# State-space heads of the first two layers: 128-token tiles in five phases, or 64-token blocks in one phase

## The chip, the cores and the metric

The kernel runs on one core of a Trainium2 chip. The metric is the device time of one execution in microseconds (us). Three executions of the kernel before took 3934.63 to 3938.2 us, median 3936.54 us. PE is the matrix engine, PEld its weight load; DVE, ACT and POOL are the vector, scalar and GpSimd engines.

## The reference, cut to what matters

The program is a four-layer network on 512 tokens of width 1024, in float32. Layers 0 and 1 mix tokens with six state-space heads, a dilated attention and a 31-tap convolution; the change lies in the state-space heads:

```python
def step(state, inp):              # per token and head; state is 64 x 64
    r_t, w_t, k_t, v_t, a_t, b_t = inp     # a = -kk, b = kk * a
    sa = einsum('bhij,bhj->bhi', state, a_t)
    state = state * w_t[:, :, None, :] + sa[..., None] * b_t[:, :, None, :] + v_t[..., None] * k_t[:, :, None, :]
    y_t = einsum('bhij,bhj->bhi', state, r_t)
    return state, y_t
# then per head: y = (y - mean) * rsqrt(var + eps) * ln_w + ln_b + bonus, times a gate
```

The kernels do it in chunks of 64 tokens. Within a chunk the effect of sa on later tokens is the inverse of a unit triangular 64 x 64 matrix, made of repeated squares and updates; between chunks a state is carried.

## The kernel before, in words

Everything is laid out with features on the 128 partitions (two heads of 64 above each other, e = 0 and 1) and tokens along the free axis; three such pairs (cc = 0 to 2) hold the six heads. `first_mixers` is called twice, once per layer, between the long weight chains, and runs one phase after another. A phase is a block in which each engine has its own list of instructions, tied by semaphores; it ends when all engines have ended.

After `rwkv_scale` (L1154: per pair a scan over tokens, the exponentials of the decays, the scaling of r, k, a, b) come, for each pair, a phase of transposes (`transposes`, L723) and one of `rwkv_pair` (L1219). The latter works on tiles of 128 tokens, in which two chunks lie, and on one head at a time: `by_tile` (L1256) is four matmuls of 128x128x128, the other head's rows being zeroed in the stationary operand (`heads_apart`, L1214) and the other chunk masked away. Scores, three rounds of squares and updates, two corners (m32, m64) and the products with the values follow each other, with DVE and ACT copying out of PSUM between them. Then `rwkv_states` (L1410) carries the state of all three pairs over eight chunks, two products and six DVE instructions each, and `rwkv_output` (L1476) makes y, its mean and variance per head and the output.

The convolution runs beside this. ACT multiplies a shifted input by one tap (`conv_terms`, L1586) and POOL adds the term to a sum (`conv_sums`, L1601): 62 taps, of which 60 are added by POOL. ACT's term k waits until POOL has added term k-4. Before, the taps are split over the three `rwkv_pair` phases, and the normalization of the convolution lies in `rwkv_states`.

A float32 matmul stands in the trace as two records, each with its weight load: `rwkv_output` issues 24 matmuls at L1489 per layer, and the trace has 48 rows. The orders below count matmuls, the trace records.

Of the kernel before, what the change touches and what calls it, by code (L numbers as in the profile page):

```python
# [12 lines left out]
ALU = mybir.AluOpType  # L13
# [4 lines left out]
P = 128  # L18
# [18 lines left out]
SHIFTED = 10  # L37
NGC = T // GC
# [4 lines left out]
def columns(widths):  # L43
# [17 lines left out]
    ("m16", P), ("m32", P), ("m64", P), ("m16T", P), ("strictT", P), ("inclT", P), ("incl32T", P), ("dist", T),  # L61
# [4 lines left out]
def constants():  # L66
# [12 lines left out]
    always = [np.eye(P), np.ones((P, P)), same(HD), col(1e-6), col(1e-12), col(64e-5), col(1e-5), col(1.0)]  # L79
    mixers = [  # L80
        below * same(16), below * (same(32) - same(16)), below * (same(64) - same(32)), (below * same(16)).T,
        (below * same(64)).T, upto * same(64), upto * same(32), dist,
# [114 lines left out]
class Core:  # L197
# [15 lines left out]
    N_TEMPS = align(NCB)  # L213
# [940 lines left out]
    def rwkv_scale(self):  # L1154
# [7 lines left out]
        names = ("chain", "sums_ready", "exps_ready", "bonus_in", "bonus_sum", "chunk_done")  # L1162
        with self.phases.phase(*names) as (block, chain, sums_ready, exps_ready, bonus_in, bonus_sum, chunk_done):
# [50 lines left out]
    def heads_apart(self):  # L1214


        return [self.pj(19), self.pj(20)], [self.pj(21), self.pj(22)], [self.mix[:, 0, :], self.mix[:, 1, :]]

    def rwkv_pair(self, cc):  # L1219

# [6 lines left out]
        fa, fb, fr, fk = self.pj(10 + cc), self.pj(13 + cc), self.pj(cc), self.pj(3 + cc)  # L1227
        At, Kt, Vt = (self.units("ring", i, 1)[:, 0, :] for i in range(3))
        Bt = self.units("arena", cc, 1)[:, 0, :]
        tok = lambda u: u.rearrange("p (n f) -> p n f", f=P)  # L1230
        self.transposes([g for src, dst in ((fa, At), (fk, Kt), (self.pj(6 + cc), Vt), (fb, Bt))
                         for g in self.to_tokens([src], tok(dst))])
        buffers = [[self.units("h", i, 1)[:, 0, :] for i in range(8)], [self.units("ring", 3 + i, 1)[:, 0, :] for i in range(8)]]
        (L, LT, L2, L2T, I, IT, O32, O64) = zip(*buffers)
        UT, W, MV = (self.units("arena", u, 1)[:, 0, :] for u in (3 + cc, 9 + cc, 33))
        KV = self.units("arena", 12 + 2 * cc, 2)
        G = self.units("arena", 18 + 2 * cc, 2)
        RKV = self.units("arena", 24 + cc, 1)[:, 0, :]
        rows = [slice(0, HD), slice(HD, P)]
        FB, FA, FK = self.heads_apart()  # L1240
        RKT = [self.units("arena", 32, 1)[:, 0, :], self.mix[:, 2, :]]
        tile = lambda u, i: u[:, i * P:(i + 1) * P]
        wide = lambda name: self.c(name, P).unsqueeze(1).to_broadcast([P, NT, P])
        names = ("scores_l", "masked_l", "masked_corners", "started", "scores_a", "scores_b", "masked_a", "masked_b", "values", "values_read",
                 "squares", "squares_copied", "updates", "updated", "corner", "corner_copied", "ends", "ends_read",
                 "by_head", "turned", "turned_copied", "term_ready", "added")
        with self.phases.phase(*names) as (block, scores_l, masked_l, masked_corners, started, scores_a, scores_b, masked_a, masked_b, values, values_read,
                                           squares, squares_copied, updates, updated, corner, corner_copied, ends, ends_read,
                                           by_head, turned, turned_copied, term_ready, added):
            @block.gpsimd  # L1250
            def _(pool):
                self.conv_sums(pool, self.conv_part(cc, RW), term_ready, added)

            @block.tensor
            def _(pe):
                def by_tile(bank, lhs, rhs, r=slice(0, P), out=slice(0, P)):  # L1256
                    for i in range(NT):
                        mm = nc.tensor.matmul(tile(banks[bank][out, :], i), tile(lhs[r, :], i), tile(rhs[r, :], i), start=True, stop=True)
                    return mm
                pe.wait_ge(by_head, 6)  # L1260
                for e in range(2):
                    by_tile(0 + e, FB[e], fa)
                    by_tile(2 + e, FA[e], fb).then_inc(scores_l, 1)
                for e in range(2):
                    by_tile(4 + e, FK[e], fa)
                    by_tile(6 + e, FB[e], fr).then_inc(scores_a, 1)
                pw = [(L, LT), (L2, L2T)]
                pe.wait_ge(masked_l, 2)
                for n in range(3):
                    (p, pt), (q, qt) = pw[n % 2], pw[(n + 1) % 2]  # L1270
                    if n:
                        pe.wait_ge(squares_copied, 4 * n)
                    for e in range(2):
                        if n == 0 and e == 1:
                            pe.wait_ge(masked_corners, 2)
                        mm = by_tile(0 + 2 * e, pt[e], p[e])
                        if n < 2:
                            mm = by_tile(1 + 2 * e, p[e], pt[e])
                        mm.then_inc(squares, 1)
                    if n == 0:  # L1280
                        for e in range(2):
                            pe.wait_ge(masked_a, e + 1)
                            by_tile(4 + e, FK[e], fr).then_inc(scores_b, 1)
                        pe.wait_ge(masked_b, 2)
                        for e in range(2):
                            for i in range(NT):
                                nc.tensor.matmul(banks[6][:, i * P + e * HD:i * P + e * HD + HD], tile(I[e], i),
                                                 tile(Vt, i)[:, e * HD:e * HD + HD], start=True, stop=True)
                        for i in range(NT):
                            for e in range(2):  # L1290
                                mm = nc.tensor.matmul(tile(banks[4][rows[e], :], i), tile(Vt, i)[:, e * HD:e * HD + HD],
                                                      tile(RKT[e], i), start=True, stop=True)
                        mm.then_inc(values, 1)
                        pe.wait_ge(started, 2)
                    pe.wait_ge(squares_copied, 4 * n + (4 if n < 2 else 2))
                    if n:
                        pe.wait_ge(updated, 2 * n)
                    for e in range(2):
                        by_tile(5 + 2 * e, q[e], IT[e]).then_inc(updates, 1)
                pe.wait_ge(updated, 6)  # L1300
                pe.wait_ge(values_read, 2)
                for e in range(2):
                    for i in range(NT):
                        mm = nc.tensor.transpose(tile(banks[4 + 2 * e], i), tile(IT[e], i), self.c("ident", P))
                    mm.then_inc(turned, 1)
                for e in range(2):
                    by_tile(e, O32[e], IT[e]).then_inc(corner, 1)
                pe.wait_ge(corner_copied, 2)
                pe.wait_ge(turned_copied, 2)
                for e in range(2):  # L1310
                    by_tile(4 + 2 * e, L[e], I[e])
                    by_tile(5 + 2 * e, I[e], L[e]).then_inc(updates, 1)
                pe.wait_ge(updated, 8)
                for e in range(2):
                    by_tile(e, O64[e], IT[e]).then_inc(corner, 1)
                pe.wait_ge(corner_copied, 4)
                for e in range(2):
                    by_tile(5 + 2 * e, I[e], L[e]).then_inc(updates, 1)
                pe.wait_ge(updated, 10)
# [936 lines left out]
```

## Time and profile before

| | us |
|---|---|
| median of three executions | 3936.54 |
| the profiled execution: its time, its span | 3933.45, 3931.7 |
| state-space part of layer 0 (`rwkv_scale` to the end of `rwkv_output`) | 266.7 |
| the same of layer 1 | 266.7 |
| of these in layer 0: scale / three pairs with transposes / states / output | 21.6 / 174.9 / 38.8 / 31.4 |

The parts follow each other without overlap, and nothing of the weight chains runs beside them, so a stage is read as a stretch of time: its length, the busy time of each engine and the clock granted to TensorE (1.00 is 2.4 GHz, 0.50 is 1.2 GHz).

### The profile page before, as it was taken

What the parts mean: (1) busy time and instruction counts of PE and PEld (TensorE: products, weight loads), DVE (VectorE), ACT (ScalarE), POOL (GpSimd) and SP (SyncE); (2) the same over time, 40 slices, a digit from 0 to 9 for tenths busy, and PEclk for the clock granted to TensorE, in tenths of its full rate; (3) what the DMA queues carried; (4) which work ended last, traced back from release to release, by engine and by line L of the source; (5) the groups of instructions that cost most, each with busy time, mean ns of one, the idle gap of its engine ahead of it and who ended that gap; (6) DMA issues with size and microseconds to landing.
All of it is one profiled execution on the core that took longest, in us unless ns stands there. A gap on an engine that the chain in (4) does not pass through costs nothing. (4 is left out here: it accounts for less than half of the span.)

```text
span 3931.7 us, 45649 instructions
## 1 busy us (share of the span) xinstructions
PE 3550.2 (90%) x17442; PEld 2914.3 (74%) x17442; DVE 1867.7 (48%) x2852; ACT 1309.2 (33%) x1921; POOL 324.5 (8%) x259
## 2 busy tenths in 40 slices
PE   7999976869999999995877999986899997789998
PEld 5888855758888888873766888865788876568887
DVE  4443335455443444335445444433566444656652
ACT  3222433423222322424433322313422331453231
POOL 0000323400000000042420000000000000210000
PEclk9999988979999999997988999995899998899999
DMA  3332300002232223320002223320222333012232
GB/s 112 97 101 92 113 12 1 1 35 97 96 105 88 96 96 103 112 71 1 1 1 68 94 98 103 122 74 1 73 98 97 100 104 121 1 44 95 98 102 81
DMA packets 73440, 295.09 MB, mean 75 GB/s; under 512 B 8144, under 2 KB 9168, under 8 KB 72144
## 3 DMA queue, kind: packets, MB, share of 16 engines
q1 hardware_dynamic: 73296, 293.09, 22.4%
q8 instruction: 101, 1.65, 0.2%
q14 instruction: 43, 0.35, 0.0%
HBM read 290.96 MB, written 2.10 MB: 75 GB/s over the span
## 5 line engine op out<-in xcount | busy, mean ns | idle before, releaser
L427 PE MATMUL bank<-src_hi,tile_hi 128*128 128x512 f32 x2720 | 1068.7, 393 | 26.2 <-DVE tile_lo L501 25.4
L428 PE MATMUL bank<-src_lo,tile_hi 128*128 128x512 f32 x2720 | 1059.3, 389 | 0.0
L429 PE MATMUL bank<-src_hi,tile_lo 128*128 128x512 f32 x2720 | 1059.2, 389 | 0.0
L501 DVE TENSOR_TENSOR tile_lo<-raw_tiles,tile_hi 128x1024 fp32r<-128x1024 f32 (+1 forms) x484 | 618.7, 1304 | 84.3 <-ACT tile_hi L453 68.1
L427 PEld LDWEIGHTS bank<-src_hi,tile_hi 128*128 128x128 f32 x2720 | 511.0, 188 | 138.7 <-DVE tile_lo L501 25.4
L428 PEld LDWEIGHTS bank<-src_lo,tile_hi 128*128 128x128 f32 x2720 | 511.2, 188 | 110.4 <-issue 5.3
L453 ACT ACTIVATE tile_hi<-raw_tiles 128x1024 fp32r<-128x1024 f32 (+1 forms) x484 | 524.6, 1112 | 199.0 <-DMA raw_tiles<-in_w_in 92.8
L429 PEld LDWEIGHTS bank<-src_hi,tile_lo 128*128 128x128 f32 x2720 | 511.1, 188 | 106.7
L427 PE MATMUL bank<-hid_hi,tile_hi 128*128 128x512 f32 x1312 | 515.1, 393 | 48.4 <-DVE tile_lo L501 48.4
L428 PE MATMUL bank<-hid_lo,tile_hi 128*128 128x512 f32 x1312 | 514.0, 392 | 0.0
L429 PE MATMUL bank<-hid_hi,tile_lo 128*128 128x512 f32 x1312 | 513.5, 391 | 0.0
L427 PEld LDWEIGHTS bank<-hid_hi,tile_hi 128*128 128x128 f32 x1312 | 248.5, 189 | 102.1 <-DVE tile_lo L501 50.5
L428 PEld LDWEIGHTS bank<-hid_lo,tile_hi 128*128 128x128 f32 x1312 | 248.7, 190 | 52.0
L429 PEld LDWEIGHTS bank<-hid_hi,tile_lo 128*128 128x128 f32 x1312 | 248.5, 189 | 52.2
L701 DVE TENSOR_TENSOR temps<-bank,temps 128x512 f32<-128x512 f32 x88 | 60.8, 691 | 405.5 <-PE bank L429 405.5
L668 DVE SCALAR_TENSOR_TENSOR x_res<-bank,x_res 128x512 f32<-128x512 f32 (+1 forms) x80 | 55.3, 691 | 414.1 <-PE bank L429 414.1
L687 ACT ACTIVATE temps<-temps 128x512 f32<-128x512 f32 x88 | 55.6, 632 | 574.9 <-DVE temps L701 574.9
L660 ACT ACTIVATE src_hi<-temps 128x512 fp32r<-128x512 f32 (+1 forms) x72 | 45.5, 632 | 554.7 <-DVE temps L672 554.7
L536 DVE TENSOR_TENSOR big<-bank,hspace 128x512 f32<-128x512 f32 x76 | 52.6, 692 | 248.9 <-PE bank L429 231.5
L1612 POOL TENSOR_TENSOR mix<-mix,masks 128x512 f32<-128x512 f32 x120 | 148.7, 1271 | 221.7 <-ACT masks L1599 221.7
L716 DVE TENSOR_TENSOR hid_lo<-temps,hid_hi 128x512 f32 (+1 forms) x132 | 91.4, 693 | 119.0 <-ACT hid_hi L691 119.0
L689 ACT ACTIVATE temps<-temps,par 128x512 f32<-128x512 f32 x44 | 31.9, 724 | 289.4 <-DVE temps L711 289.4
(380 smaller groups left out, 3569.9 us busy)
## 6 DMA issues: line engine op xcount, KB each, us to landing
raw_tiles<-in_gu SPq DMA_DIRECT2D x264, 512.0 KB, 3.4
raw_tiles<-in_down SPq DMA_DIRECT2D x96, 704.0 KB, 4.1
raw_tiles<-in_w_in SPq DMA_DIRECT2D x46, 512.0 KB, 3.4
masks<-in_masks SPq DMA_DIRECT2D x4, 2108.0 KB, 8.3
raw_tiles<-in_w_out SPq DMA_DIRECT2D x16, 512.0 KB, 3.5
raw_tiles<-in_a_in SPq DMA_DIRECT2D x16, 512.0 KB, 3.5
raw_tiles<-in_w_mem SPq DMA_DIRECT2D x16, 512.0 KB, 3.4
raw_tiles<-in_a_out SPq DMA_DIRECT2D x8, 512.0 KB, 3.8
```

The source lines that it names most:

```text
L427: nc.tensor.matmul(bank, wh, hi[:, kk, 0:p.n], start=(kk == 0), stop=False)
L428: nc.tensor.matmul(bank, wh, lo[:, kk, 0:p.n], start=False, stop=False)
L429: mm = nc.tensor.matmul(bank, wl, hi[:, kk, 0:p.n], start=False, stop=last and (p.kind == "gated" or s == p.h - 1))
L453: nc.scalar.activation(self.tile_hi[:, t, 0:kc * P], self.tile_raw[:, t, 0:kc * P], ACT.Copy).then_inc(hi_ready, 1)
L501: v.tensor_tensor(self.tile_lo[:, t, 0:kc * P], self.tile_raw[:, t, 0:kc * P], self.tile_hi[:, t, 0:kc * P].bitcast(F32), ALU.subtract).th ...
L536: v.tensor_tensor(p.dst[:, p.place(i), 0:p.n], p.banks_of(banks, k)[0], self.rstd_of(p), ALU.mult).then_inc(bank_free, 1)
L660: nc.scalar.activation(chunk(self.src_hi, i), self.temps[:, 4 + k % 2, :], ACT.Copy).then_inc(own["next_hi"], 1)
L668: v.scalar_tensor_tensor(chunk(self.x, i), p.banks_of(self.banks, k)[0], float(p.factor), chunk(self.x, i), ALU.mult, ALU.add).then_inc(ow ...
L687: nc.scalar.activation(one, one, ACT.Silu).then_inc(own["activated"], 1)
L701: v.tensor_tensor(gate, bank[0], rstd, ALU.mult).then_inc(own["gate_ready"], 1)
L716: v.tensor_tensor(chunk(self.hid_lo, i), prod, chunk(self.hid_hi, i).bitcast(F32), ALU.subtract).then_inc(own["hid_ready"], 1)
L1612: self.nc.gpsimd.tensor_tensor(acc[:, c, :], acc[:, c, :], slots[k % 4], ALU.add).then_inc(added, 1)
```

## The change

`rwkv_pair`, `rwkv_states` and `rwkv_output` and the transposes between them become one phase, `rwkv_chunks`. All work is on blocks of 64 tokens and 64 features. A product is 16 matmuls of 64x64x64 (8 chunks, 2 heads); the first head uses partitions 0 to 63 of input and output, the second 64 to 127, so they lie in different quarters of the array. PE's list interleaves the first head of a product with the second head of the product before it, chunk by chunk, in different PSUM banks. 33 named products are made for each of the three pairs, pair after pair within a name; 27 of them share a ring of five banks, where a product waits until the copy of the fifth before it is made. 13 names are copied out by ACT, the rest by DVE: 19 groups of three full-width instructions, among them the copies of the turned squares (sq2t, sq4t) and of the score-weighted values (mv). Squares with the identity take the place of the transposes. The carried state is six steps (`step`), each three matmuls per head half and one DVE addition. POOL first scales b, k and the identity by the decay at the chunk's end (9 instructions), then adds taps. 16 taps (14 additions) are moved ahead into `rwkv_scale`, the other 46 lie in the new phase, three or four after each ACT group. The convolution's normalization moves behind the last product. The masks are 64 wide instead of 128.

```diff
+FIRST_TAPS = 16
...
-    ("m16", P), ("m32", P), ("m64", P), ("m16T", P), ("strictT", P), ("inclT", P), ("incl32T", P), ("dist", T),
+    ("m16", CH), ("m32", CH), ("m64", CH), ("m16T", CH), ("strictT", CH), ("inclT", CH), ("ident2", CH), ("incl32T", P), ("dist", T),
...
+        taps = self.conv_part(0, FIRST_TAPS)
...
-                for pair in self.heads_apart():
-                    for e in range(2):
-                        nc.gpsimd.memset(pair[e][(1 - e) * HD:(2 - e) * HD, :], 0.0)
+                self.conv_sums(pool, taps, term_ready, added)
...
+                    self.conv_terms(act, taps, 6 * c, 6, term_ready, added)
...
+    RWKV_PRODUCTS = ("lt", "l", "v", "a", "sq2", "sq2t", "ka", "up1", "sq4", "sq4t", "mv", "up2", "sq8", "g", "up3", "rk", "turn", "c1",
+                     "b", "up4", "up4t", "k", "c2", "up5", "n1", "u", "w", "q", "mt", "n2", "y1", "y2", "y3")
+    RWKV_VECTOR = ("lt", "l", "started", "o32", "o64", "sq2t", "ka", "up1", "sq4t", "mv", "up2", "g", "up3", "rk", "up4", "up4t", "up5", "q", "mt")
+    RWKV_SCALAR = ("v", "a", "sq2", "sq4", "sq8", "turn", "c1", "b", "k", "c2", "u", "w", "n2")
+
+    def rwkv_chunks(self):
...
+        ring = [(name, cc) for name in self.RWKV_PRODUCTS if name not in ("l", "n1", "n2", "y1", "y2", "y3") for cc in range(RW)]
+        bank_of = {at: banks[i % 5] for i, at in enumerate(ring)}
...
+        taps = self.conv_part(FIRST_TAPS, TAPS * CV)
...
+                for cc in range(RW):
+                    nc.gpsimd.tensor_tensor(chunks(Be[cc]), chunks(Fb[cc]), end(cc), ALU.mult).then_inc(ends_scaled, 1)
+                    nc.gpsimd.tensor_tensor(chunks(Ke[cc]), chunks(Fk[cc]), end(cc), ALU.mult).then_inc(ends_scaled, 1)
+                    nc.gpsimd.tensor_tensor(chunks(MT[cc]), mask("ident2"), end(cc), ALU.mult).then_inc(ends_scaled, 1)
+                self.conv_sums(pool, taps, term_ready, added)
...
+                def half(at, lhs, rhs, e, c):
+                    first = at[0] not in ("n2", "y2", "y3")
+                    r = rhs[rows[e], :] if rhs.shape[1] == CH else chunk(rhs, c)[rows[e], :]
+                    return nc.tensor.matmul(chunk(bank_of[at], c)[rows[e], :], chunk(lhs, c)[rows[e], :], r,
+                                            start=first and c == 0, stop=(c == NCH - 1), skip_group_check=True)
+
+                def product(name, cc, lhs, rhs, skip=0):
+
+                    nonlocal behind
+                    at = (name, cc)
+                    if at in ring and ring.index(at) >= 5:
+                        last = ring[ring.index(at) - 5]
+                        if last[0] in self.RWKV_SCALAR:
+                            pe.wait_ge(kept_a, in_a(*last))
+                        else:
+                            pe.wait_ge(kept_v, in_v(*last))
+                    for c in range(NCH):
+                        if c >= skip:
+                            half(at, lhs, rhs, 0, c)
+                        if behind is not None and c >= behind[3]:
+                            mm = half(*behind[0:3], 1, c)
+                    if behind is not None:
+                        mm.then_inc(multiplied, 1)
+                    behind = (at, lhs, rhs, skip)
...
+                def step(e, c):
+
+                    if c > 1:
+                        pe.wait_ge(added_to[e], c - 1)
+                    for cc in range(RW):
+                        mm = nc.tensor.matmul(scan_banks[e][rows[e], cc * CH:(cc + 1) * CH], chunk(MT[cc], c)[rows[e], :],
+                                              N[rows[e], cc, (c - 1) * CH:c * CH], start=(cc == 0), stop=(cc == RW - 1), skip_group_check=True)
+                    mm.then_inc(stepped[e], 1)
...
+                for cc in range(RW):
+                    pe.wait_ge(kept_v, in_v("l", cc))
+                    product("sq2", cc, LT[cc], L[cc])
+                for cc in range(RW):
+                    product("sq2t", cc, L[cc], LT[cc])
...
+                for c in range(1, NCH - 1):
+                    for e in range(2):
+                        step(e, c)
+                    if c <= 2:
+                        product("y1", c, V[c], RK[c])
+                    elif c <= 5:
+                        product("y2", c - 3, L2T[c - 3], G[c - 3])
...
+                    product("y3", cc, states_behind(cc), Fr[cc], skip=1)
+                finish()
+                self.conv_mean(pe, taps, added, conv_mean)
...
+                def keep(name, to):
...
+                        act.wait_ge(multiplied, made(name, cc))
+                        nc.scalar.activation(to[cc], bank_of[name, cc][:, :], ACT.Copy).then_inc(kept_a, 1)
+                    more = 3 if name in ("v", "a", "sq2") else 4
+                    self.conv_terms(act, taps, term, more, term_ready, added)
...
+                def copied(name, to):
+                    for cc in range(RW):
+                        dve.wait_ge(multiplied, made(name, cc))
+                        v.tensor_copy(to[cc], bank_of[name, cc][:, :]).then_inc(kept_v, 1)
...
+                copied("sq2t", L2T)
...
+                copied("sq4t", LT)
+                copied("mv", KA)
...
+                        to = N[rows[e], :, c * CH:(c + 1) * CH]
+                        v.tensor_tensor(to, to, scan_banks[e][rows[e], 0:RW * CH].rearrange("p (c f) -> p c f", c=RW), ALU.add).then_inc(added_to[e], 1)
...
-        for cc in range(RW):
-            self.rwkv_pair(cc)
-        self.rwkv_states()
-        self.rwkv_output()
+        self.rwkv_chunks()
```

PE's list at the start of layer 0's work on the heads, before (`hspace` holds the first head's matrices, `ring` the second's):

```order
L1258 MATMUL bank0<-big_66 128x128 [waits by_head_10]
L1258 MATMUL bank0<-big_66 128x128 x3
L1258 MATMUL bank2<-big_66 128x128 x4
L1258 MATMUL bank1<-big_66 128x128 x4
L1258 MATMUL bank3<-big_66 128x128 x4
```

and PE's list at the same place after (`big` holds the inputs of both heads):

```order
L1279 MATMUL bank0<-big_66 64x64 x8
L1279 MATMUL bank1<-big_66 64x64
L1279 MATMUL bank0<-big_66 64x64
L1279 MATMUL bank1<-big_66 64x64
L1279 MATMUL bank0<-big_66 64x64
L1279 MATMUL bank1<-big_66 64x64
```

Whole runs of four 128-wide matmuls into one bank have become 64-wide ones that alternate between two banks, one head half each.

PE's list in the carrying of the state, before, two chunks of it (L1435 multiplies by the state, L1445 updates it):

```order
L1435 MATMUL bank0<-arena_63 64x128 [waits loaded_1]
L1435 MATMUL bank0<-arena_63 64x128 x2
L1445 MATMUL bank2<-ring_65,arena_63 128x128 [waits tile_split_3]
L1445 MATMUL bank2<-ring_65,arena_63 128x128 x2
L1435 MATMUL bank1<-arena_63 64x128 [waits loaded_1]
L1435 MATMUL bank1<-arena_63 64x128 x2
L1445 MATMUL bank3<-ring_65,arena_63 128x128 [waits tile_split_3]
L1445 MATMUL bank3<-ring_65,arena_63 128x128 x2
```

PE's list there after, one step of both head halves (the 16 matmuls of an output product stand between two such steps; bank1 and bank2 hold the halves):

```order
L1313 MATMUL bank1<-arena_63,ring_65 64x64 [waits src_hi_ready_3]
L1313 MATMUL bank1<-arena_63,ring_65 64x64
L1313 MATMUL bank1<-arena_63 64x64
L1313 MATMUL bank2<-arena_63,ring_65 64x64 [waits src_ready_3]
L1313 MATMUL bank2<-arena_63,ring_65 64x64
L1313 MATMUL bank2<-arena_63 64x64
```

Two dependent groups per chunk have become one.

## Rows read from the trace of the kernel before

**Rows 1.** The page: busy time, share of the span, instructions; TensorE's clock in 40 slices.

```profile
PE 3550.2 (90%) x17442; PEld 2914.3 (74%) x17442; DVE 1867.7 (48%) x2852; ACT 1309.2 (33%) x1921; POOL 324.5 (8%) x259
PEclk9999988979999999997988999995899998899999
```

**Rows 2.** Stages: from:to, length, busy us (records) by engine; clock; DMA.

```profile
core 0: us, PE busy (x) PEld busy (x) DVE busy (x) ACT busy (x) POOL busy (x), PEclk, DMA share, GB/s
593.40:615.00 21.60, 6.22 (x6) 1.50 (x6) 21.45 (x36) 5.00 (x9) 3.31 (x6) 0.50 0.00 0
615.00:673.10 58.10, 47.68 (x392) 45.28 (x392) 24.34 (x40) 23.81 (x40) 22.33 (x18) 0.94 0.00 1
789.90:828.70 38.80, 24.90 (x98) 17.07 (x98) 25.85 (x48) 7.78 (x9) 0.00 (x0) 0.66 0.00 0
828.70:860.10 31.40, 20.62 (x108) 16.91 (x108) 10.55 (x15) 7.97 (x11) 0.00 (x0) 0.66 0.00 1
593.40:860.10 266.70, 193.48 (x1388) 170.01 (x1388) 132.38 (x219) 93.95 (x151) 77.61 (x66) 0.84 0.00 1
1835.70:2102.40 266.70, 193.49 (x1388) 168.55 (x1388) 132.39 (x219) 94.09 (x152) 77.67 (x66) 0.84 0.00 1
```

**Rows 3.** Timeline of PE: start, length of the run, instruction, records.

```profile
641.39 1.95 PE L1258 MATMUL bank<-hspace 128*128 128x128 f32 x16
...
2070.35 10.48 PE L1489 MATMUL bank<-big,arena 128*128 128x64 f32 x48 [0.92 <-PEq L113]
2080.76 5.32 PE L1494 MATMUL bank<-arena,ring 128*64 128x128 f32 x48
...
2681.13 6.71 PE L1803 MATMUL bank<-arena 32*64 32x128 f32 x128 [1.05 <-PEq L113]
...
544.61 0.49 PE L962 MATMUL bank<-big 64*128 64x128 f32 x4
```

**Rows 4.** Timeline of PE, single records in two column halves.

```profile
669.82 0.27 PE L1326 MATMUL bank<-hspace,ring 128*64 128x128 f32 x1
669.83 0.27 PE L1326 MATMUL bank<-ring 128*64 128x128 f32 x1
669.93 0.27 PE L1326 MATMUL bank<-hspace,ring 128*64 128x128 f32 x1
```

**Rows 5.** PE alone in stretches: length, busy us (records), clock, DMA.

```profile
640.00:670.00 30.00, 24.22 (x206) 1.00 0.00 1
2070.30:2080.80 10.50, 10.45 (x50) 0.50 0.00 0
2683.20:2687.70 4.50, 4.50 (x76) 0.50 0.00 0
```

**Rows 6.** Timelines of DVE, ACT and POOL in layer 0.

```profile
628.04 0.68 DVE L1372 TENSOR_TENSOR hspace<-bank,masks 128x512 f32<-128x512 f32 x1
628.64 0.68 DVE L1373 TENSOR_TENSOR hspace<-bank,masks 128x512 f32<-128x512 f32 x1
...
791.33 0.55 DVE L1456 TENSOR_TENSOR ring<-bank,arena 64x384 f32<-64x384 f32 x1 [0.96 <-PE bank L1435]
...
645.66 2.55 ACT L1599 ACTIVATE masks<-arena,par 128x512 f32<-128x512 f32 x4
...
810.43 1.28 ACT L1651 ACT_TABLE_LOAD   x1
...
646.45 9.87 POOL L1612 TENSOR_TENSOR mix<-mix,masks 128x512 f32<-128x512 f32 x8 [6.22 <-ACT masks L1599]
```

**Rows 7.** Timelines of ACT, DVE, PE: the ends of `rwkv_scale` and `rwkv_output`.

```profile
611.08 0.61 ACT L1178 ACTIVATE hspace<-hspace 128x512 f32<-128x512 f32 x1
...
614.26 0.68 DVE L1212 TENSOR_TENSOR arena<-bank,big 128x512 f32<-128x512 f32 x1
...
859.30 0.69 DVE L1533 TENSOR_TENSOR mix<-hspace,big 128x512 f32<-128x512 f32 x1
...
844.01 2.41 PE L1500 MATMUL bank<-hspace,const 128*128 128x512 f32 x5
```

More of the change, by code:

```diff
@@ L1264, in _ @@
[L1264 to L1319, printed above, removed]
@@ L1327, in _ @@
-                for o in range(2):
-                    for i in range(NT):
-                        mm = nc.tensor.matmul(tile(banks[2 + o], i), tile(Kt[rows[o], :], i), tile(Vt[rows[o], :], i), start=True, stop=True)
-                mm.then_inc(ends, 1)
+                behind = None
+                def half(at, lhs, rhs, e, c):
[3 more added lines that the diff above has]
+                                            start=first and c == 0, stop=(c == NCH - 1), skip_group_check=True)
@@ new lines, in finish @@
+                def finish():
+                    nonlocal behind
+                    for c in range(behind[3], NCH):
+                        mm = half(*behind[0:3], 1, c)
+                    mm.then_inc(multiplied, 1)
+                    behind = None
+                def step(e, c):
[5 more added lines that the diff above has]
+                    mm.then_inc(stepped[e], 1)
@@ L1358, in _ @@
-                act.wait_ge(ends, 1)
-                nc.scalar.activation(UT, banks[0][:, :], ACT.Copy)
-                nc.scalar.activation(W, banks[1][:, :], ACT.Copy).then_inc(ends_read, 1)
+                term = 0
+                def keep(name, to):
+                    nonlocal term
+                    for cc in range(RW):
+                        act.wait_ge(multiplied, made(name, cc))
+                        nc.scalar.activation(to[cc], bank_of[name, cc][:, :], ACT.Copy).then_inc(kept_a, 1)
+                    more = 3 if name in ("v", "a", "sq2") else 4
+                    self.conv_terms(act, taps, term, more, term_ready, added)
+                    term += more
@@ new lines, in _ @@
+                keep("v", V)
+                keep("a", A)
+                keep("sq2", L2)
+                keep("sq4", L)
+                keep("sq8", L2)
+                keep("turn", L2T)
+                keep("c1", L)
+                keep("b", B)
+                keep("k", K)
+                keep("c2", L2)
+                keep("u", L)
+                keep("w", L2T)
+                keep("n2", [N[:, cc, :] for cc in range(RW)])
+                assert term >= len(taps)
+                self.conv_squares(act, conv_centred, conv_squared)
@@ new lines, in increased @@
+                def increased(name, to, old, ready):
+                    for cc in range(RW):
+                        dve.wait_ge(multiplied, made(name, cc))
+                        if ready is not None:
+                            dve.wait_ge(kept_v, in_v(ready, cc))
+                        v.tensor_tensor(to[cc], old[cc], bank_of[name, cc][:, :], ALU.add).then_inc(kept_v, 1)
+                masked("lt", LT, "m16T")
+                masked("l", L, "m16")
+                for cc in range(RW):
+                    dve.wait_ge(kept_v, in_v("lt", cc))
+                    v.tensor_tensor(chunks(IT[cc]), chunks(LT[cc]), mask("ident2"), ALU.add).then_inc(kept_v, 1)
@@ L1579, in _, with conv_part @@
                     nc.vector.tensor_copy(lora[r, k, :], self.par1[r, PC1["lora"]:PC1["lora"] + RW * P])
[L1581 to L1584 removed]
+    def conv_part(self, first, last):
+        return [(j, c) for j in range(TAPS) for c in range(CV)][first:last]
     def conv_terms(self, act, taps, first, n, term_ready, added):
```

408 lines of the change are left out of this document (180 added, 228 removed).

## The prediction

> **What bounds the kernel now.** I read the page first, then the stages, then the timelines of PE at the kinds of matmul that the change is made of, and last the ends of the stages on the other engines. The page shows PE busy in 90% of the span [rows 1]; most of that is weight products that the change does not touch. The stages show where it acts: from the start of the scaling to the end of the output 266.7 us in either layer, 533 in all, with nothing of the weight chains beside it [rows 2]. A microsecond saved there is one saved in the total. Within them, one pair with its transposes takes 58.1 us, PE busy in 47.7 of it, DVE in 24.3, ACT in 23.8, POOL in 22.3: PE bounds it, with gaps where it waits for copies. In the carrying of the state (38.8 us) PE and DVE are each busy for 25 us: a chain of hops [rows 2]. The clock granted is 0.94 in the pair, 0.66 in the two stages behind it, 0.50 in the scaling.
>
> **What PE's small matmuls cost.** A float32 matmul is two records. At L1258 16 records of a 128-wide stationary and 128 moving columns take 1.95 us at full clock [rows 3, 5], 0.112 each; a product for one head over 512 tokens is four matmuls, 0.89 us, and 1.8 for both heads. At half clock, 48 records at L1489 with a 128-wide stationary and 64 moving columns take 10.48 us [rows 3, 5]: without the tail of the last, 0.214 each. Halving the moving side gains nothing there, the load sets the pace. At L1494 the same number, two column halves running together, takes 5.32 us [rows 3]: 0.21 per pair of records with 128 moving columns. The same pairs at full clock start 0.11 apart [rows 4].
>
> The new matmul is 64 wide on both sides. Half the load of L1489 gives 0.107 us per record at half clock, half the stream of L1494 gives the same; at full clock 0.053. The first head's quarter and the second's are interleaved. That such quarters run together is shown by L962, where two row halves alternate: four records in 0.49 us, of which a lone one takes about 0.27, so 0.22 for what would be 0.33 in file [rows 3]; and by L1803, 32x64 tiles with 128 moving columns, at 0.052 each [rows 3], a quarter of the 0.214 of a full record at that clock. So a product of 16 matmuls is 16 pairs of records: **1.71 us at half clock, 0.86 at full clock**. If the quarters did not overlap it would be 3.42 and 1.71.
>
> **Which clock.** This decides. The dense stream at L1489, PE busy 10.45 of 10.5 us, stays at 0.50 to its end; that at L1803, busy all of 4.5 us, too [rows 5]. Neither is a stream of 128-wide, 128-column matmuls. The products of that kind at L1258 hold 1.00 though PE is busy in only 24.2 of 30 us [rows 5]. The new stream resembles the first two (64 columns, partial tiles), and begins behind the scaling, at 0.50 [rows 2]. I take half clock throughout the phase.
>
> The Trainium skill, "TensorE: Matmul & The Clock Gate", section "Why this matters for your kernels", asks only that TensorE be kept busy without gaps for the full clock. By that rule the new phase, dense on PE, would run at 2.4 GHz; the two dense stretches at 0.50 in this trace disagree, and I follow them. It is the first rival.
>
> **The change part by part, for one layer.**
> - *Scaling.* POOL's memsets go (hidden, at nothing); 14 additions come, eight take 9.87 us [rows 6], so 17.3. The first can start when ACT has made its terms behind the first exponentials, about 599.5, so POOL ends near 617; DVE ends at 614.9 [rows 7]. Cost +2.2. ACT's terms (six are 3.8 us at 2.55 for four [rows 6]) fit between the exponentials. PE starts the new phase at 617.5.
> - *Products up to n2.* 30 names for three pairs, 90 products, and one slot more since a product's second half goes beside the next: 91 x 1.71 = 155.6. What lies beside: DVE 19 groups of three at a pitch of 0.60 [rows 6], 34 us, among them the nine copies sq2t, sq4t and mv, 5.4 us; ACT 39 copies and 46 terms at no more than 0.64, 54 us; POOL 9 scalings and 46 additions at 1.24, 68 us, which holds ACT back through the wait on term k-4. All are under half of 155.6, so they cost nothing at this clock; the tightest place, c2 behind four terms, stalls PE by half a microsecond. The last copy by ACT follows at 617.5 + 155.6 + 1 = 774.
> - *Carrying.* A step is 6 records in each quarter, 0.64, and with the output product behind it 2.35; five of them 11.8, which hides DVE's additions (64x384 takes 0.55 [rows 6], these have half the columns, some 0.35 each). The sixth stands alone: 0.64 and latency and two additions, 1.8. Then y3, seven chunks, three and the rest: 6.6. The last product is made at 774 + 11.8 + 1.8 + 6.6 = 794.
> - *End.* Before, the end of the products to the last write took 844.0 to 860.0 [rows 7], 16.0. Now the convolution's mean and variance are queued between (two and two matmuls of 512 columns on PE, about 2 us at half clock) and its Ln and Exp with two table loads of 1.28 [rows 6], 3.9 on ACT ahead of the heads' own. 16 + 5.9 = 22. The end is at 816.
> - *Gone:* six changes of phase, the transposes, the zeroing copies; they are in the stretch replaced.
>
> So 860.1 becomes 816, 44 less; both layers 88. Against the profiled execution 3933.45 - 88 = 3845; the median lies 3.1 above it, 3848. For stalls that I do not see I add 2: **3850 us**. The masks are narrower by 320 columns of 4216; their load runs beside the projection and is taken at nothing.
>
> The new kind of record stands nowhere in this trace. Its bounds by the nearest rows: 0.052 per record in file (L1803's pace for each single record would be 1.66 per product, nearly the same as chosen), at best 0.053 per pair, at worst 0.214 per pair. I take 0.107.
>
> The Trainium skill, "TensorE: Matmul & The Clock Gate", section "Wait — 56ns, not 53.3ns?", knows a floor of about 62 ns per matmul when its decoding runs in microcode. By it 32 records would be 2.0 us a product and each layer some 30 us longer, 3910 in all. L1803's 128 records in 6.71 us are under this floor, so the sum does not use it.
>
> **Rivals.**
> 1. *Full clock, in whole or part.* For it: PE has no gaps; L1494 is also a pair of partial tiles, and the 512-column records behind it take 0.48 each [rows 7], near four times the 0.107 of 128 columns at full clock, so the clock rose in it. Against it: the two stretches at 0.50. Then 91 x 0.856 = 78; POOL's 68 are just under it and ACT's waits for POOL begin to show. Carrying 6 x 1.2, y3 3.3, end 20: the layer ends near 728, 132 less; total 3936.5 - 264 = 3673. With half the phase at either clock 3760.
> 2. *The quarters do not overlap* (slower than before). The place is every product: e = 0 and e = 1 take turns. 3.42 a product adds 155.6 up to n2 and some 15 behind it: the layer ends at 986, 126 later than before, total 4188. It decides from 2.2 us a product on: (860 - 816)/91 = 0.48 above 1.71. For it: no row shows matmuls halved in rows and columns both, each quarter writing its own bank. Against it: L962 and L1803.
> 3. *A smaller cost in every record* (a floor between issues, stalls at the ring of banks): 10 to 25% on each product, 15 to 40 us a layer: 3880 to 3930, little or nothing gained.
>
> **How the numbers follow.** Forecast 0.58, own range 3825 to 3880. Rival 1 0.22 (half of it part-way, 3720 to 3825). Rival 3 0.10, rival 2 0.10. The range for eight in ten leaves out rival 2 and most of the fully fast case: 3690 to 3895. A measurement of this kernel tells 0.2%, 8 us. Faster is the forecast, rival 1 and most of rival 3: 0.87; the same 0.03; slower 0.10.
>
> **What would show it.** In the profile after: the clock row at 0.5 from the scaling to the end of the heads; the new matmul line at 32 records per 1.71 us; PE busy nearly all of 155 us, POOL done in the middle of the phase; the phase from 617.5 to 816. If the clock there is 1.0, rival 1 has it. If 32 records take over 2.2 us at half clock, rival 2 or 3. If PE waits for ACT's copies while ACT waits for POOL, I have the cover wrong. A difference outside the two stretches of heads would also make this wrong.

## The result, and the profile after

The changed kernel takes 3719.3 us (median of four runs, 3717.4 to 3720.2), the kernel before 3935.6 beside it: a ratio of 0.9449, 95% interval 0.9433 to 0.9466. The gain is 216 us where the forecast had 86 (3936 to 3850). The time is outside the forecast's own range (3825 to 3880) and inside the wide one (3690 to 3895); it lies between rival 1's two figures, 3673 for the full clock and 3760 for half of the phase at either, and the clock below is the full one. The step that failed is "I take half clock throughout the phase".

The page of the kernel after, engines and clock row (the lines of [rows 1]):

```profile
PE 3388.8 (91%) x21174; PEld 2781.2 (75%) x21174; DVE 1784.9 (48%) x2662; ACT 1283.4 (35%) x1879; POOL 347.9 (9%) x265
PEclk9999997989999999997989999967999997899999
```

PE executes 3732 records more and is busy 161 us less. POOL is busy 23 us more: 18 scalings of 1.04 us came and the memsets went, but the convolution's additions also took 160.6 us instead of 148.7 with a like number of them, which comes back below.

The stages of the kernel after, with the columns of [rows 2]: scaling; start of the products; products up to n2; carrying and output products; end; then the whole in either layer.

```profile
593.40:627.90 34.50, 6.22 (x6) 1.51 (x7) 33.50 (x36) 15.21 (x25) 22.65 (x14) 0.50 0.00 0
627.90:631.30 3.40, 3.38 (x49) 3.40 (x51) 0.00 (x0) 0.00 (x0) 3.12 (x4) 0.50 0.02 5
631.30:721.20 89.90, 85.97 (x2852) 84.49 (x2849) 38.66 (x57) 49.34 (x85) 61.55 (x51) 1.00 0.02 4
721.20:734.50 13.30, 12.51 (x337) 11.41 (x338) 6.29 (x15) 0.51 (x1) 1.27 (x1) 1.00 0.02 4
734.50:754.20 19.70, 6.95 (x17) 2.77 (x15) 10.96 (x16) 15.63 (x20) 0.00 (x0) 0.75 0.00 0
593.40:754.20 160.80, 115.03 (x3254) 103.58 (x3254) 89.41 (x124) 80.70 (x130) 88.59 (x69) 0.85 0.01 3
1731.00:1890.60 159.60, 114.53 (x3254) 103.98 (x3254) 89.59 (x124) 80.70 (x130) 90.10 (x69) 0.84 0.01 3
```

Three things are to be read here. The clock is 0.50 for the first 3.4 us of the products and 1.00 from there to the end of the output products. The scaling takes 34.5 us where [rows 2] had 21.6. And the stretch of 266.7 us is now 160.8 and 159.6; the two differences, 105.9 and 107.1, are 213 of the 215 us that the span lost, so nothing of weight happened elsewhere. Of layer 0's 105.9 us, 78.5 are busy time of PE (193.48 before, 115.03 now) and 27.4 its idle time. What the single phase brings without the 64-wide blocks was not run apart.

The pace of a product, from PE's timeline of single records in the middle of the phase (compare [rows 4]):

```profile
640.83 0.22 PE L1279 MATMUL bank<-masks,big 64*64 64x64 f32 x1
640.83 0.22 PE L1279 MATMUL bank<-arena 64*64 64x64 f32 x1
640.89 0.22 PE L1279 MATMUL bank<-masks,big 64*64 64x64 f32 x1
640.89 0.22 PE L1279 MATMUL bank<-arena 64*64 64x64 f32 x1
```

Two quarters, one of each head, start at the same moment and the next two some 0.058 us later (the rows round it to 0.06): they do run together, and 16 such pairs are 0.93 us a product.

Where the scaling lost its 13 us, VectorE's timeline in the second pair of heads:

```profile
601.30 1.65 DVE L1196 TENSOR_TENSOR_SCAN hspace<-masks,arena 128x512 f32<-128x512 f32 x1
602.87 1.42 DVE L1197 TENSOR_SCALAR hspace<-arena,par 128x512 f32<-128x512 f32 x1
604.20 1.75 DVE L1199 TENSOR_TENSOR hspace<-hspace,arena 128x512 f32<-128x512 f32 x1
605.87 0.68 DVE L1201 SCALAR_TENSOR_TENSOR big<-hspace,big 128x512 f32<-128x512 f32 x1
...
608.94 1.76 DVE L1210 TENSOR_TENSOR big<-big,hspace 128x512 f32<-128x512 f32 x1
610.62 1.75 DVE L1211 TENSOR_TENSOR big<-big,hspace 128x512 f32<-128x512 f32 x1
612.29 1.23 DVE L1212 COPY small<-hspace 128x8 f32<-128x8 f32 x1
613.44 0.68 DVE L1214 TENSOR_TENSOR arena<-bank,big 128x512 f32<-128x512 f32 x1
```

and GpSimd's in the same time:

```profile
599.04 6.36 POOL L1608 TENSOR_TENSOR mix<-mix,masks 128x512 f32<-128x512 f32 x4 [34.58 <-ACT masks L1595]
608.34 9.92 POOL L1608 TENSOR_TENSOR mix<-mix,masks 128x512 f32<-128x512 f32 x6 [2.94 <-ACT masks L1595]
```

A VectorE instruction of 512 columns with two inputs in SBUF takes 0.68 us while GpSimd is idle (605.4 to 608.3) and 1.75 while it adds; a copy of 8 elements takes 1.23. L1214, with one of its inputs in a PSUM bank, takes 0.68 while GpSimd adds. GpSimd's additions take 1.6 each instead of the 1.23 of [rows 6]. The Trainium skill, "SBUF — State Buffer", section "Who interferes with whom", says that a VectorE instruction with two SBUF inputs, or a copy or scalar operation in a two-port mode, and a GpSimd instruction that reads SBUF block each other for the length of an instruction. By that rule, which the prediction did not weigh, these steps had to wait; the trace agrees, with 0.4 (the scan) to 1.1 us more at a time.

### The profile page after: what moved, and what is told of

The parts are those of the page before. It is cut to its first block and busy times, and to the rows that moved or that the text cites. A ratio compares the mean times of both kernels' runs of the same rounds, so it can differ in the third digit from the quotient of the medians.

```text
span 3716.8 us, 52829 instructions
## 1 busy us (share of the span) xinstructions
PE 3388.8 (91%) x21174; PEld 2781.2 (75%) x21174; DVE 1784.9 (48%) x2662; ACT 1283.4 (35%) x1879; POOL 347.9 (9%) x265
## 5 line engine op out<-in xcount | busy, mean ns | idle before, releaser
L1608 POOL TENSOR_TENSOR mix<-mix,masks 128x512 f32<-128x512 f32 x120 | 160.6, 1375 | 134.9 <-ACT masks L1595 134.9
```

Source lines behind the costliest of these rows:

```text
L1608: self.nc.gpsimd.tensor_tensor(acc[:, c, :], acc[:, c, :], slots[k % 4], ALU.add).then_inc(added, 1)
```

## The experiments

The theories. **Clock:** a dense stream of these quarters, two in flight, brings TensorE to 2.4 GHz and keeps it there; the rows that the prediction followed are of another kind of stream. Its rival: [rows 5] showed stretches too short, or with too idle a past, for a rise. **Contention:** the 13 us of the scaling are VectorE and GpSimd in each other's way. Its rivals: the instruction's form, or something behind it. **Copies:** where the nine copies stand makes no difference. The edits are shown in short form. The kernel before of the first four runs took 3936.4 us; of the runs e5 to e8 3936.2; of the last two 3936.0.

**e5, the other kind, four times as long.** In the kernel before, ahead of the products at its line 1489:

```diff
+for _ in range(3):
+    for cc in range(RW):
+        for c in range(NCH):
+            matmul(banks[3 + cc][:, chunk c], state(c)[:, cc, :], pj(cc)[:, chunk c])
```

> The kernel before, with the 24 products of the output with a 128-wide stationary and 64 moving columns (48 records, 10.48 us at a granted clock of 0.50) made three times more in each layer, ahead of themselves, into free banks. If the kind of matmul keeps the clock at 0.50 (my step in the prediction), the 144 added records take 0.214 each: 31 us a layer, 3936 + 62 = 3998, and the granted clock stays 0.50 through some 42 us. If the stretch was only too short or its ahead too idle, the clock goes to 1.00 within it, a record then takes about 0.11, and the layer grows by 16 to 25 us: 3968 to 3986.

Measured in one run 3999.1 us, 63 more. PE's timeline and the clock in the stretch:

```profile
832.38 30.95 PE L1490 MATMUL bank<-big,arena 128*128 128x64 f32 x144 [0.92 <-PEq L113]
863.13 10.45 PE L1494 MATMUL bank<-big,arena 128*128 128x64 f32 x48
873.51 5.29 PE L1499 MATMUL bank<-arena,ring 128*64 128x128 f32 x48
```

```profile
840.00:850.00 10.00, 10.00 (x49) 10.00 (x48) 0.00 (x0) 0.00 (x0) 0.00 (x0) 0.50 0.00 0
...
860.00:870.00 10.00, 10.00 (x49) 10.00 (x48) 0.00 (x0) 0.00 (x0) 0.00 (x0) 0.50 0.01 2
870.00:880.00 10.00, 10.00 (x68) 9.06 (x68) 2.19 (x4) 0.00 (x0) 0.00 (x0) 0.57 0.00 0
```

PE is busy without a gap for 41 us at 0.50, and the clock rises only near the end of the column halves of L1499 behind it. So what the prediction said of L1489 was sound, and the length of that stretch was not its fault. The rule of the Trainium skill that the prediction weighed ("TensorE: Matmul & The Clock Gate", section "Why this matters for your kernels": busy without gaps gives the full clock) does not hold for this stream.

**e6, quarters in turn at the same place.**

```diff
+for _ in range(6):
+    for cc in range(RW):
+        for c in range(NCH):
+            for r in (rows 0:64, rows 64:128):
+                matmul(banks[3 + cc][r, chunk c], state(c)[r, cc, r], pj(cc)[r, chunk c])
```

> The kernel before, with 288 pairs of quarter matmuls (64 rows, 64 stationary and 64 moving columns, the two heads' quarters in turn, as the changed kernel's products) in each layer ahead of the output's products, into free banks; nothing reads them. If such a stream brings the clock up by itself, it does so within a few us here too, at the same place where the other kind stayed at 0.50; a pair then takes 0.058: 17 us a layer and the output's own 48 records go faster, 5 less: 3936 + 24 to 34 = 3965. If the rise in the changed kernel came from something else in its phase, the pairs stay at 0.107: 31 us a layer, 3998.

Measured in one run 3957.4 us, 21 more. PE's timeline, then the stretches with the clock:

```profile
828.98 19.00 PE L1492 MATMUL bank<-big,arena 64*64 64x64 f32 x576 [0.92 <-PEq L113]
847.90 5.57 PE L1496 MATMUL bank<-big,arena 128*128 128x64 f32 x48
853.41 2.84 PE L1501 MATMUL bank<-arena,ring 128*64 128x128 f32 x48
```

```profile
830.00:840.00 10.00, 10.00 (x296) 10.00 (x294) 0.00 (x0) 0.00 (x0) 0.00 (x0) 0.83 0.02 5
840.00:850.00 10.00, 10.00 (x293) 9.93 (x288) 0.00 (x0) 0.00 (x0) 0.00 (x0) 1.00 0.01 3
```

At the same place, behind the same stage, the quarters bring the clock up, and 576 records take 19.0 us where 144 of the other kind took 30.95. The L1496 behind them (L1489 of the kernel before) runs at 5.57 us instead of 10.48: already at full clock, it keeps it for that long. So at this place the kind of stream sets the clock, not the phase around it. The added time is below the expected 24 to 34. In a layer the pairs cost 19.0 where 17 were expected, and behind them 4.9 us at L1496, which was expected, and 2.0 at L1501, which was not, come off; 2.1 more come off outside the heads, where the matmuls of L1803 ran at full clock here (more on this below).

**e7, the same quarters in file.** In the changed kernel:

```diff
-for c in range(NCH):
-    half(at, lhs, rhs, 0, c)
-    half(*behind[0:3], 1, c)
+for c in range(NCH):
+    half(at, lhs, rhs, 0, c)
+for c in range(NCH):
+    half(*behind[0:3], 1, c)
```

> The changed kernel with the two heads' quarter matmuls of a product no longer in turn: all eight of the first head, then all eight of the second head of the product before. The numbers are the same. If the pace of 0.058 us for two quarters comes from their running together, a product takes 32 single records: 1.87 us at full clock instead of 0.93, 85 us a layer over 91 products and some 8 behind them, about 3905 in all; at half clock 3.4 us, and over 4150. If quarters run at 0.029 each in any order, nothing changes: 3719. Rival on the clock: with half the work in flight it falls to 0.50.

Measured 4060.1 us, ratio to the kernel before 1.0313 [1.0294, 1.0332]: slower than before. The first products, and two stretches, of its trace:

```profile
628.43 8.85 PE L1279 MATMUL bank<-big 64*64 64x64 f32 x96 [5.12 <-PEq L115]
```

```profile
634.00:660.00 26.00, 26.00 (x316) 26.00 (x315) 8.99 (x15) 4.22 (x7) 7.44 (x7) 0.50 0.01 1
755.00:785.00 30.00, 30.00 (x363) 30.00 (x361) 1.38 (x2) 10.89 (x19) 10.07 (x9) 0.50 0.01 2
```

The same instructions, in another order: in these stretches PE is never idle, the clock stays at 0.50 for over 200 us, a record starts every 0.084 us (16 of them between 723.91 and 725.25) and a product takes 2.68 us, 2.9 times the 0.93. A record in file at half clock costs less than the 0.107 that I had for a pair, so my 3.4 us a product, and over 4150, were too high; the sign of rival 2 was right for this order.

**e9, column halves of full height.** As e5, each added product cut into two matmuls on the column halves of its stationary, in turn.

```diff
+            for r in (slice(0, 64), slice(64, 128)):
+                matmul(banks[3 + cc][r, chunk c], state(c)[:, cc, r], pj(cc)[:, chunk c])
```

> As the kernel with the 24 products repeated three times (3999 us, clock 0.50 to the end, 31 us a layer), but each added product is two matmuls on the column halves of its stationary (128 rows, 64 wide, 64 moving columns), the halves in turn: 288 records instead of 144 for the same products. Since the quarters in turn rose to 1.00 and the same quarters in file stayed at 0.50, I expect that two tiles in flight are what brings the clock up, whether they share rows or not: 144 pairs at 0.107 for the first few us, then 0.058: 9 to 11 us a layer, and the 48 records behind them at full clock, 5 less: 3936 + 8 to 14 = 3947. The rival, that it is the halved rows: the pairs stay at 0.107, 15 us a layer, 3967; or halves of full height don't run together: 0.17 to 0.21 a pair and more, 3985 or above.

Measured in one run 3946.2 us, 10 more. PE's timeline:

```profile
833.38 10.99 PE L1491 MATMUL bank<-big,arena 128*64 128x64 f32 x288 [0.92 <-PEq L113]
844.30 5.57 PE L1495 MATMUL bank<-big,arena 128*128 128x64 f32 x48
```

The same products as e5's in 10.99 us instead of 30.95. Rows need not be split; two column halves in turn are enough.

**e10, the split alone.** The kernel before with its own 24 products at L1489 so split, nothing added.

```diff
-nc.tensor.matmul(banks[cc][:, chunk c], state(c)[:, cc, :], pj(cc)[:, chunk c])
+for r in (slice(0, 64), slice(64, 128)):
+    nc.tensor.matmul(banks[cc][r, chunk c], state(c)[:, cc, r], pj(cc)[:, chunk c])
```

> The kernel before with only its own 24 products of the output split in this way, nothing repeated: 10.48 us become 144 / 3 = 48 pairs, 5.1 at half clock or some 4 with the clock rising in it, and the 48 records behind them, 4.87 us before, start at full clock and take 2.8. So 6 to 8 us less a layer: 3936 - 14 = 3922. If the clock does not rise in it, 5 us a layer: 3926. If splitting does not help: 3936.

Measured 3916.7 us, ratio 0.9955 [0.9941, 0.9968]: 19 us less, by one more loop, and more than the 14 expected; 2.1 of them lie outside the heads, at the matmuls of L1803 (below). Its products, and the clock in them:

```profile
833.05 5.39 PE L1490 MATMUL bank<-big,arena 128*64 128x64 f32 x96 [0.92 <-PEq L113]
838.20 2.87 PE L1495 MATMUL bank<-arena,ring 128*64 128x128 f32 x48
```

```profile
833.10:838.20 5.10, 5.10 (x97) 0.50 0.01 3
```

The 10.47 us of L1489 in layer 0 became 5.39 at half clock: this part is the halves running together, not the clock. The clock rises at their end, and the records behind them take 2.87 us where they took 4.87.

**e1, no taps beside the scaling.** In the changed kernel FIRST_TAPS = 0, and four or five terms behind each group of ScalarE's copies instead of three or four.

```diff
-FIRST_TAPS = 16
+FIRST_TAPS = 0
-    more = 3 if name in ("v", "a", "sq2") else 4
+    more = 4 if name in ("v", "a", "sq2") else 5
```

> The 16 taps of the convolution that the changed kernel puts beside the scaling go into the products' phase (all 62 there, four or five terms behind each group of ScalarE's copies). Contention theory: VectorE's steps with both inputs in SBUF take 1.75 us instead of 0.68 because GpSimd adds at the same time; without its additions the scaling takes 21.7 us again and TensorE's first product starts near 616.5 instead of 627.9, so 11 us less in each layer, 3697 us in all. The rival, that the scaling is longer for another reason (its own new waits, ScalarE's terms behind the exponentials are gone too but cost only 3.8), gives a gain of 0 to 4 us a layer, 3712 to 3719. A second rival: GpSimd with 9 scalings and 62 additions (86 us in a phase of 93) holds the copies back and gives all of it back: 3719 or slower.

Measured 3706.5 us (ratio to before 0.9421 [0.9409, 0.9434]), 13 less than the changed kernel's 3719.3. VectorE at the rows shown above:

```profile
600.98 0.68 DVE L1199 TENSOR_TENSOR hspace<-hspace,arena 128x512 f32<-128x512 f32 x1
...
604.65 0.69 DVE L1210 TENSOR_TENSOR big<-big,hspace 128x512 f32<-128x512 f32 x1
...
605.85 0.17 DVE L1212 COPY small<-hspace 128x8 f32<-128x8 f32 x1
```

With GpSimd's additions gone, every step is back at its time, and VectorE's last step in the scaling starts 20.8 us after its first, as in the kernel before, instead of 33.3. But 22 us were expected and 13 came. PE's waits in the phase of layer 0 of e1 (us in total, times, longest) show where the rest went:

```profile
PE bank L1279 <- ACT arena L1431: 6.7, 5, 2.8
```

and its stretches with the clock:

```profile
656.00:670.00 14.00, 14.00 (x488) 14.00 (x484) 6.22 (x9) 7.65 (x14) 8.18 (x7) 1.00 0.02 5
670.00:684.00 14.00, 10.62 (x305) 10.40 (x301) 4.13 (x6) 10.03 (x17) 14.00 (x13) 0.88 0.01 2
684.00:698.00 14.00, 11.64 (x346) 11.50 (x342) 2.06 (x3) 9.57 (x16) 13.13 (x12) 0.88 0.02 4
```

PE waits for ScalarE's copies behind the longer groups of terms (2.1 us so in the changed kernel, 6.7 here), GpSimd is busy all the time, and in the stretches with gaps the granted clock is 0.88: a wait seems to be paid a second time through the clock.

**e4, the terms where nobody waits.** As e1, with the terms spread by hand.

```diff
-    more = 4 if name in ("v", "a", "sq2") else 5
+    more = TERMS_BEHIND[name]   # v 4, a 4, sq2 9, sq4 9, sq8 9, turn 0, c1 3, b 5, k 2, c2 5, u 2, w 6, n2 4
```

> As the kernel without taps beside the scaling, but the 62 terms stand where ScalarE is not followed by a copy that TensorE waits for: 9 each behind sq2, sq4 and sq8, none behind turn, two or three behind c1, k and u. If the stalls that remain in the products (15 us of issue time before the first matmul of a product in two layers, 10 for ScalarE's copies) are due to copies queued behind terms, 3 to 5 us a layer less than with the even spread: 3688 us. If GpSimd's 86 us are the bound, the spread changes nothing: as the first kernel, 3697.

Measured 3688.8 us (3687.7 to 3691.2), ratio to before 0.9377 [0.9364, 0.9390]: the fastest version here, 30.5 less than the changed kernel. The same wait and stretch in it:

```profile
PE bank L1281 <- ACT arena L1433: 1.5, 3, 0.8
```

```profile
670.00:684.00 14.00, 13.46 (x462) 13.33 (x459) 4.12 (x6) 10.26 (x19) 12.40 (x10) 1.00 0.02 5
```

Eighteen us lie between e1 and e4 with equal work on every engine, so GpSimd's 86 us of work, the second rival of e1's expectation, are not the bound. Of these nine us a layer, PE's waits for copies account for 5.8 (8.8 in e1, 3.0 here); that the rest is the lower clock is an estimate.

**e2, another form.** In the scaling, L1199, L1210 and L1211:

```diff
-v.tensor_tensor(r, r, e_in, ALU.mult)
+v.scalar_tensor_tensor(r, r, 1.0, e_in, ALU.mult, ALU.mult)
```

> Three TENSOR_TENSOR instructions a pair in the scaling (the sums before, r and k) become SCALAR_TENSOR_TENSOR with a factor of 1, same result; in the trace that form took 0.68 to 0.69 us beside GpSimd's additions. If the form decides who is slowed, some six of them come down from 1.75 to 0.69: 6 us less in each layer, 3707 us. If any step of VectorE with two SBUF inputs waits for the addition that GpSimd has begun, and the quick ones only stood where GpSimd was idle, nothing changes: 3719, and SCALAR_TENSOR_TENSOR is then seen at 1.7 us.

Measured 3718.0 us (3715.8 to 3720.4): no change. In its trace the new form is as slow where GpSimd adds:

```profile
603.63 1.75 DVE L1199 SCALAR_TENSOR_TENSOR hspace<-hspace,arena 128x512 f32<-128x512 f32 x1
...
608.37 1.75 DVE L1210 SCALAR_TENSOR_TENSOR big<-big,hspace 128x512 f32<-128x512 f32 x1
```

The theory of the form falls: the quick ones had stood where GpSimd was idle.

**e8, the taps beside the scaling in the kernel before.**

```diff
 def rwkv_scale: pool
+    pool.wait_ge(cleared, 6)
+    self.conv_sums(pool, taps[0:16], term_ready, added)
 def rwkv_scale: act, behind the exponentials of pair c
+    self.conv_terms(act, taps[0:16], 6 * c, 6, term_ready, added)
```

> The kernel before with this one part of the change: the first 16 taps of the convolution stand beside the scaling (terms on ScalarE behind the exponentials, 14 additions on GpSimd), and the three pairs share the other 46. If two engines reading SBUF in turn is what stretches the scaling, it does so here: 11 to 13 us a layer more ahead of the first pair. The pairs, in which TensorE sets the pace, gain at most a little from their fewer terms (0 to 3 us a layer): 3936 + 16 to 26 = 3952 to 3962. The rival, that in the changed kernel the scaling was longer for what is behind it, gives 3936 or less.

Measured 3960.8 us (ratio 1.0061 [1.0047, 1.0074]): 25 more, 12 a layer. Stretches of its trace:

```profile
593.40:615.00 21.60, 4.15 (x4) 1.00 (x4) 21.53 (x26) 11.10 (x18) 15.95 (x13) 0.50 0.00 0
615.00:628.00 13.00, 2.07 (x2) 0.50 (x2) 13.00 (x11) 4.12 (x7) 11.51 (x8) 0.50 0.00 0
628.00:686.00 58.00, 47.76 (x392) 45.36 (x392) 24.11 (x40) 20.00 (x34) 18.55 (x15) 0.94 0.00 1
```

The scaling ends near 628 as in the changed kernel, and the first pair, now with fewer terms, takes the 58 us of [rows 2]: nothing is given back, since PE sets the pace there. This part of the change alone makes the scaling 12 us longer in a layer, as much as its absence took off the scaling in e1; there half of it was lost again to waits in the products, and 13 us in all were left.

**e3, the nine copies on ScalarE.** In the changed kernel sq2t, sq4t and mv go from VectorE's list to ScalarE's.

```diff
-    copied("sq2t", L2T)   copied("sq4t", LT)   copied("mv", KA)
+    keep("sq2t", L2T, 0)  keep("sq4t", LT, 0)  keep("mv", KA, 0)
```

> The nine copies sq2t, sq4t and mv, which the change puts on VectorE, go to ScalarE, ahead of its terms. My theory is that TensorE sets the pace there and either engine hides 5.4 us of copies in a layer: within 8 us of 3719. The rival is that their place is a part of the gain: ScalarE then comes late with sq4 and the terms behind it, and each group of copies (3 x 0.6 us) shows once in the phase, 5 us a layer or more: 3730 or slower.

Measured 3719.5 us (3714.0 to 3721.6), ratio to before 0.9452 [0.9439, 0.9465] against 0.9449: no difference. The part of the change that moves copies brings and costs nothing.

## Why the prediction was wrong, step by step

- **Which clock: failed.** The forecast took 1.71 us a product, half clock throughout. The phase ran at 2.4 GHz but for its first 3.4 us, 0.93 a product. The last copy of n2 ends 93 us after the first product, not 157: 63 us a layer, 127 of the 131 us between forecast and result; the other misses about cancel. The step put the new stream with L1489 and L1803 because of "64 columns, partial tiles". e5 shows that L1489 stays at half clock however long it lasts, e6 and e9 that a stream with the same 64 columns rises when two tiles are in flight, e7 that the changed kernel's own quarters stay down in file. What told them apart stood in the profile: L1494, also a pair of tiles, near whose end the clock rose. I had it as an argument for the rival and gave it too little.
- **The second witness, L1803: misread.** [rows 5] shows its last 4.5 us only. The kernel before, then the same matmuls in the kernel after (L1802), with PE's columns alone:

```profile
2681.00:2683.00 2.00, 1.87 (x54) 1.00 0.06 16
2683.00:2685.00 2.00, 2.00 (x47) 0.55 0.00 0
```

```profile
2466.68 4.59 PE L1802 MATMUL bank<-arena 32*64 32x128 f32 x128 [1.05 <-PEq L115]
```

```profile
2466.70:2471.20 4.50, 4.50 (x128) 1.00 0.01 4
```

It began at full clock and fell after 2 us, with PE busy; in the kernel after it ran at full clock throughout, and so it did in e6 and e10 (4.6 us), while e5 and e9 have 6.7 again. These 2.1 us are what the span lost outside the heads. So it was no case of a kind that stays at half clock, and its 0.052 a record, which the prediction set beside 0.214 at half clock, is a mean over both clocks (0.034 at full clock, 4.59 us for 128). Why the same matmuls came out either way stays open.
- **The quarters overlap: right.** Sixteen pairs a product, as argued from L962 and L1803 (from the latter with the mixed figure). The pitch at full clock is 0.058 and not 0.0535, 7 us a layer over rival 1's 78. Rival 2 did not come; e7 shows it was a matter of the order alone.
- **Scaling +2.2: mis-sized, +12.6.** The first product comes at 627.9, not 617.5, 10.4 later. I counted the additions on GpSimd as work beside VectorE; e1, e2 and e8 show that they are in each other's way, in either form tried.
- **Copies and terms hidden: right for the nine copies** (e3), nearly for the terms. VectorE and ScalarE are busy 39 and 49 of 90 us, yet PE waits about 4 us in a phase that is half as long as forecast, and e4 against e1 shows how sharp that becomes. "They cost nothing at this clock" was true with its condition; the condition failed.
- **Carrying, output products: 20.2 forecast, some 12 measured**, at the clock of the phase. VectorE's additions are 0.37 each as estimated, a step 1.28 us.
- **End: 22 forecast, 21.4 measured.**

Together for layer 0: 816 + 10.4 (scaling) - 63.4 (products) - 8.5 (carrying and output products) - 0.6 (end) = 753.9; the last write ends at 754.2. Where e5, e6 and e9 are single runs, their differences of 10 to 63 us lie well beyond the spread of the kernel before (3929.8 to 3939.8 over three sets of nine runs), except that e9's 10 us is near it; its verdict rests on the timeline. Why the clock answers to one stream and not to another that keeps PE as busy is not shown by these runs, only which do; two tiles in turn also means more records in a microsecond, and no run holds one of the two still.

## What to carry to other kernels

Before pricing a new kind of small matmul, look at the granted clock of each kind near it, from the start of its stretch and at more than one place, and compare also by how many tiles run at once. With 64 columns, two column halves or two quarters in turn ran almost three times as fast as the same work undivided or in file, and running together alone makes a factor of 1.6 (in file 2.68 a product, in turn at half clock some 1.7) to 1.9 (e10) of that, the clock the rest; e10 gets half a per cent from it with one loop. It is not the tiles alone: L1258, one 128-wide tile at a time with 128 columns, holds 1.00 in [rows 5]. Never count work on GpSimd as hidden beside VectorE when both read SBUF; put it where VectorE reads one input from PSUM, as L1214 does at 0.68 us. Where a wait is on TensorE's path, order the other engine's optional work so that no copy stands behind it: equal work, 18 us.

## What the runs showed of the hardware that was not expected

- Matmul with a 128-wide stationary and 64 moving columns, one at a time: 0.50 for 41 us with PE always busy, 0.215 us a record; column halves in turn: 10.99 us for what took 30.95.
- Quarters of 64x64 with 64 columns: in turn at full clock 0.058 us a pair, in file at 0.50 0.084 a record.
- VectorE and GpSimd, 512 columns: 0.68 alone, 1.75 beside GpSimd's additions; 0.46 becomes 1.42, the scan's 1.23 becomes 1.65, an 8-element copy's 0.17 becomes 1.23; GpSimd's 1.23 becomes 1.6 and more.
- A clock that is up stays up in a stream that would not bring it up: L1496 of e6, 48 records in 5.57 us against 10.48.
- A clock that is up can fall while PE is busy: L1803 in the kernel before, from 1.00 to 0.50 after 2 us; the same matmuls hold 1.00 for all of 4.6 us in the kernel after.
